# V projection of an encoder layer: eight block products made into seven, with sums of x and w on the other engines

## The reference, cut to what matters

```python
qkv = (x @ w_qkv).reshape(bsz, rows, GRID_W, 3, NA_HEADS, HEAD_DIM)
v = qkv[:, :, :, 2]                       # V of all 16 heads: x (1024 x 1024) times w (1024 x 1024)
...                                       # scores with position bias, softmax over 8 x 16 neighbours
out = pr @ v;  x = layer_norm(ALPHA * x + out @ w_o)     # then gate, embedding, MLP, second norm
```

## Time and profile before

| | us |
|---|---|
| median of 3 runs (1221.72 to 1223.22) | 1222.62 |
| profiled execution, its own time | 1221.3 |
| its span, first to last instruction | 1219.5 |
| V stage, first V matmul to first Q/K matmul | 6.06 to 100.07 |

### The profile page before, as it was taken

One profiled execution on the slowest core, in us unless ns is written; L12 is line 12 of the kernel. 1 busy time (PEld: TensorE's weight loads), 2 busy tenths in 40 slices (PEclk: granted clock), 3 DMA queues, 4 the chain that ended last, 5 costly groups with the idle time before them and its releaser, 6 DMA issues.

```text
span 1219.5 us, 16871 instructions
## 1 busy us (share of the span) xinstructions
PE 1207.0 (99%) x5756; PEld 1012.8 (83%) x5756; DVE 815.8 (67%) x1586; ACT 588.0 (48%) x1139; POOL 211.9 (17%) x264
## 2 busy tenths in 40 slices
PE   9999999999999999999999999999999999999997
PEld 7887888888888888888888888888888888888886
DVE  3311666666667677769677677776764575588786
ACT  3311667677677633244444444444453433333571
POOL 0320555555554433200000000000000000000000
PEclk9999999999999999999999999999999999999999
DMA  8644333433244776683556556465579775778533
GB/s 259 203 127 123 92 94 76 125 111 117 85 121 146 247 221 201 191 312 113 176 211 240 189 208 229 171 239 192 205 250 379 282 271 215 262 242 307 190 104 104
DMA packets 166068, 232.57 MB, mean 191 GB/s; under 512 B 11872, under 2 KB 91872, under 8 KB 164576
## 3 DMA queue, kind: packets, MB, share of 16 engines
q1 hardware_dynamic: 165840, 231.37, 57.4%
q10 hardware_dynamic: 144, 0.13, 0.0%
HBM read 155.83 MB, written 67.29 MB: 183 GB/s over the span
## 4 chain that ended last, share of the span: by engine, by line
PE 96%; DVE 1%; DMA 1%; issue 1%; SPq 0%; ACT 0%; DVEq 0%; ACTq 0%
PE bank L2808 25%; PE bank L2776 25%; PE bank L1263 14%; PE bank L1403 7%; PE bank L1293 7%; PE bank L2732 6%; PE bank L1359 3%; PE bank L1338 3%; PE bank L1324 3%; PE bank L1396 1%; PE bank L1279 1%; PE bank L294 1%; DMA ple_embedding<-embedding_place 0%; DMA k_lo_twice<-k_lo_twice 0%; DMA x_chunk<-in_x 0%
## 5 line engine op out<-in xcount | busy, mean ns | idle before, releaser
L830 POOL TENSOR_TENSOR probabilities<-probabilities,total_reciprocal 128x384 f32<-128x384 f32 (+1 forms) x128 | 99.0, 774 | 153.7 <-DVE total_reciprocal L1148 153.5
L2776 PE MATMUL bank<-x_combination,weight_parts 128*128 128x512 f32 x504 | 118.5, 389 | 0.0
L963 ACT ACTIVATE probabilities<-negated_scores,negated_max 128x384 f32<-128x384 f32 (+1 forms) x128 | 75.5, 590 | 83.0 <-DVE negated_max L1142 82.9
L2776 PEld LDWEIGHTS bank<-x_combination,weight_parts 128*128 128x128 f32 x504 | 94.6, 188 | 19.6
L1263 PE MATMUL bank<-act_T_hi,w_qkv_hi 128*128 128x512 f32 x256 | 102.6, 401 | 0.0
L1263 PE MATMUL bank<-act_T_lo,w_qkv_hi 128*128 128x512 f32 x256 | 100.4, 392 | 0.0
L1263 PE MATMUL bank<-act_T_hi,w_qkv_lo 128*128 128x512 f32 x256 | 100.4, 392 | 0.0
L1142 DVE CUSTOM_DVE_ANT_0 negated_scores<-bank,bias_inner 128x384 f32<-128x384 f32 x96 | 53.2, 554 | 46.5 <-issue 46.0
L2776 PE MATMUL bank<-act_T_hi,weight_parts 128*128 128x512 f32 x240 | 77.3, 389 | 0.0
L2134 ACT ACTIVATE hidden_staging<-hidden_staging 128x512 f32<-128x512 f32 x48 | 30.3, 632 | 94.9 <-DVE hidden_staging L2474 94.9
L2808 PE MATMUL bank<-x_combination,hidden_parts_odd 128*128 128x512 f32 (+1 forms) x324 | 73.1, 381 | 0.0
(11 more groups left out here) (244 smaller groups left out, 2906.8 us busy)
## 6 DMA issues: line engine op xcount, KB each, us to landing
hidden_combinations<-hidden_staging SPq DMA_DIRECT2D x112, 256.0 KB, 2.2
w_ff_in<-in_w_ff SPq DMA_DIRECT2D x27, 1024.0 KB, 7.9
weight_raw<-in_w_ff SPq DMA_DIRECT2D x25, 1024.0 KB, 5.6
weight_raw<-hidden_combinations SPq DMA_DIRECT2D x14, 1024.0 KB, 5.5
hidden_in<-hidden_combinations SPq DMA_DIRECT2D x14, 1024.0 KB, 5.5
v_parts<-v_tile_parts SPq DMA_DIRECT2D x16, 512.0 KB, 3.8
weight_raw<-in_na_w_qkv SPq DMA_DIRECT2D x16, 512.0 KB, 3.8
v_hi_lo<-v_parts SPq DMA_DIRECT2D x8, 1024.0 KB, 5.6
```

The costliest lines, as they stand in the source:

```text
L830: nc.gpsimd.tensor_tensor(prob[:, u % 4, 0:n], prob[:, u % 4, 0:n], recip[:, u % 4:u % 4 + 1].to_broadcast([P, n]), ALU.mult).then_inc(pro ...
L963: nc.scalar.activation(prob[:, u % 4, 0:n], score[:, u % 2, 0:n], ACT.Exp, scale=-1.0, bias=nmax[:, u % 4:u % 4 + 1], accum_out=total[:, u ...
L2776: mm = nc.tensor.matmul(bank, w1_part(wp, u, p)[:, k, :], x_part(ap, p, k), start=(k == 0 and n == 0 and p in (1, 5, 6)), stop=(k == KH4 - ...
```

## The change

x is cut in two by two blocks (inner half by token half), w in two by two (inner half by column half). In place of the eight block products, seven (`V_PRODUCTS`, in the order 1, 2, 5, 6, 7, 3, 4), four of them of sums or differences of blocks. Each product is 4 token tiles (`QUARTER`) by 4 chunks (`KC2`) by 3 passes.

- Product 1 is x's chunks 0 to 3 of the first 512 tokens with `w11`, product 2 chunks 4 to 7 with `w12`; these run as x arrives, chunk by chunk, four tiles instead of six. x is turned one chunk further ahead, into four banks instead of two.
- x operands: ACT also copies the turned chunk raw (`x_raw_copy`); DVE makes `x_sum1` for product 5 and `x_sum3` for product 7; POOL makes those of products 6 and 4, from four chunks each.
- w operands: DVE makes `w21 + w22` for 5 and `w12 - w11'` for 3; POOL makes `w21' = w11 - w21` for 7 and `w11' = w22 - w21'` for 6. `w12` is loaded a second time.
- Every sum is then split: high on ACT, low on DVE, the low parts of x for 7 and 4 on POOL.
- Products 6, 7, 4 share four banks and 5, 3 the other four; DVE adds the banks to the kept product 1 (`v_total`), which gives three quarters of V from SBUF. POOL makes two quarters' low parts.
- SP: no wait on `first_lo` for w's second half; the first pair's Q and K weights come after products 6 and 3; `k_twice(0, 0)` comes before `load_v(0, 0)`.

The core of the diff:

```diff
+V_PRODUCTS = (1, 2, 5, 6, 7, 3, 4)
...
 # POOL
+            for k in range(KC2):
+                pool.wait_ge(x_raw, x_turns(KC2 + k, 1))
+                pool.wait_ge(t1_sum, x_turns(k, 1))
+                pool.wait_ge(x3_sum, k + 1)
+                difference(x_sum_raw[6](k), x_sum_raw[6](k), x_sum_raw[5](k), v_operand_sum)
+                pool.wait_ge(v_operand_sum, 2 * k + 1)
+                difference(x_sum_raw[4](k), x_sum_raw[4](k), x_sum_raw[6](k), v_operand_sum)
+            for k in range(KC2):
+                pool.wait_ge(s1_sum, k + 1)
+                pool.wait_ge(first_lo, w_parts(1, k))
+                difference(w21[0][:, k, :], w11[0][:, k, :], w21[0][:, k, :], v_operand_sum)
+                pool.wait_ge(v_operand_sum, X_SUMS_FIRST + 2 * k + 1)
+                difference(w11[0][:, k, :], w22[0][:, k, :], w21[0][:, k, :], v_operand_sum)
+            for p in (7, 4):
+                for k in range(KC2):
+                    pool.wait_ge(t_hi, x_sum_parts(p, k))
+                    difference(x_part[p](1, k), x_sum_raw[p](k), x_part[p](0, k).bitcast(F32), v_operand_sum)
...
 # DVE
+            for k in range(KC):
+                x_low(k, 0); x_low(k, 1)
+                w_v_low(1 + k // KC2, k % KC2)
+                if k < KC2:
+                    x_sum_first(k, 0); x_sum_first(k, 1)
+                elif k < KC - 1:
+                    x_sum_third(k - KC2)
+            for k in range(KC2):
+                w_sum_first(k)
+                x_sum_low(5, k)
+                w_v_low(5, k)
+                if k == 0:
+                    x_sum_third(KC2 - 1)
+            for n in range(QUARTER):
+                v_low(n)
+            for k in range(KC2):
+                w_sum_fourth(k)
+                w_v_low(6, k)
+                x_sum_low(6, k)
+            for k in range(KC2):
+                w_v_low(7, k)
...
 # PE
+            def v_product(p):
+                for k in range(KC2):
+                    pe.wait_ge(first_lo, w_parts(p, k))
+                    if p in (5, 6):
+                        pe.wait_ge(t_lo, x_sum_parts(p, k))
+                    elif p in (7, 4):
+                        pe.wait_ge(v_operand_sum, X_SUMS_FIRST + x_sum_parts(p, k))
+                    for i in range(QUARTER):
...
+                        v_products(p, i, k)
-            for n in range(FIRST_TILES, V_TILES):
-                v_tile(n)
+            for p in V_PRODUCTS[2:]:
+                v_product(p)
```

More of the change, by code:

```diff
@@ L468, in attention @@
         x_lo = sem("x_lo_done")
+        x3_sum = w4_sum = recip_done
         block = S.block
[L473 to L484, removed]
         def at(name, shape, offset, dt=F32):
             return nc.alloc_sbuf_tensor_at(name, shape, dt, offset=offset)
+        BLOCK = 4 * KC2 * HALF
@@ new lines, in attention @@
+        w_sum1 = raw_and_low("w_v_sum1", [P, KC2, HALF], prob_at)
+        v_first = [at(f"v_product1_{i}", [P, HALF], place)[:, :] for i, place in
+                   enumerate([inner_at + 4 * HALF * i for i in range(QUARTER - 1)] + [score_at])]
+        v_one_five = at("v_products1_5", [P, QUARTER, HALF], prob_at)
+        v_one_six = at("v_products1_6", [P, QUARTER, HALF], prob_at + BLOCK)
+        x_part = {1: lambda part, k: S.act[part][:, k, 0:HALF], 2: lambda part, k: S.act[part][:, KC2 + k, 0:HALF],
+                  3: lambda part, k: S.act[part][:, KC2 + k, HALF:T],
+                  5: lambda part, k: (x_sum_hi[0], x_sum1[1])[part][:, k, :],
+                  6: lambda part, k: x_sum42[1][:, k, HALF:T] if part else x_sum_hi[1][:, k, :],
+                  7: lambda part, k: (x_sum_hi[0], x_sum3[1])[part][:, k, :],
+                  4: lambda part, k: x_sum42[1][:, k, 0:HALF] if part else x_sum_hi[1][:, k, :]}
@@ L652, in _ @@
             sp.sem_inc(out_stored, 16)
[L653 to L656, removed]
+            for m in range(KC):
+                sp.wait_ge(*(chunk_there(m + 4) if m < 4 else second_w_there(m - 4)))
+                load_w_v(m // 2 + KC2 * (m % 2), 1).then_inc(chunk_in[m % 4], 16)
             for c in range(GC):
@@ L845, in copy_bias, with difference, v_low @@
                 nc.gpsimd.tensor_copy(full, src).then_inc(bias_ready, 1)
[L847 to L853, removed]
+            def difference(out, a, b, count):
+                nc.gpsimd.tensor_tensor(out, a, b, ALU.subtract).then_inc(count, 1)
+            def v_low(n):
+                pool.wait_ge(v_hi, n + 1)
+                parts = v_place_of(n)
+                difference(parts[:, :, 1, :], v_source(n), parts[:, :, 0, :].bitcast(F32), v_operand_sum)
+            for k in range(KC2):
[15 more added lines that the diff above has]
+                    difference(x_part[p](1, k), x_sum_raw[p](k), x_part[p](0, k).bitcast(F32), v_operand_sum)
+            for n in range(QUARTER, 2 * QUARTER):
+                v_low(n)
+            for i in range(W_LOWS):
+                split(K_, 0, i)
+            for n in range(2 * QUARTER, 3 * QUARTER):
+                v_low(n)
+            for i in range(W_LOWS):
+                split(Q_, 0, i)
+            pool.wait_ge(v_hi, V_TILES)
+            pool.wait_ge(v_lo, 2 * QUARTER)
             pool.wait_ge(mask_loaded, 16)
@@ new lines, in x_raw_copy, with v_copy @@
+            def x_raw_copy(k, t):
+                act.wait_ge(x_turned, x_turns(k, t))
+                if k == 0 and t:
+                    act.wait_ge(first_step, 2)
+                src = x_chunk_T(k, t)
+                nc.scalar.activation(x_raw_dest(k, t), src if k >= KC2 else src[:, :, QUARTER:GROUPS, :], ACT.Copy)\
+                    .then_inc(x_raw, 1)
+            def v_copy(i):
+                act.wait_ge(v_full, v_done(1, i))
+                nc.scalar.activation(v_first[i], v_first_bank(i), ACT.Copy).then_inc(v_copied, 1)
@@ L1030, in _ @@
                     split(*piece)
-            for i in range(V_PLACES):
+            for i in range(V_COUNTS):
                 act.wait_ge(v_stored[i], V_STORED)
@@ new lines, in w_sum_first, with x_sum_third, w_sum_fourth @@
+            def w_sum_first(k):
+                for half in range(2):
+                    dve.wait_ge(*second_w_there(2 * k + half))
+                nc.vector.tensor_tensor(w_raw[5][:, k, :], w21[0][:, k, :], w22[0][:, k, :], ALU.add).then_inc(s1_sum, 1)
+            def x_sum_third(k):
+                dve.wait_ge(x_raw, x_turns(KC2 + k, 1))
+                nc.vector.tensor_tensor(x_sum_raw[7](k), x_sum_raw[6](k), x_sum_raw[7](k), ALU.subtract).then_inc(x3_sum, 1)
+            def w_sum_fourth(k):
+                dve.wait_ge(w_first_in, 32)
+                dve.wait_ge(v_operand_sum, X_SUMS_FIRST + 2 * (k + 1))
+                nc.vector.tensor_tensor(w12[0][:, k, :], w12[0][:, k, :], w11[0][:, k, :], ALU.subtract).then_inc(w4_sum, 1)
@@ new lines, in v_total @@
+            def v_total(p, i):
+                dve.wait_ge(v_full, v_done(p, i))
+                out, a, bank = {5: (v_one_five[:, i, :], v_first[i], v_second_bank), 6: (v_one_six[:, i, :], v_first[i], v_first_bank),
+                                7: (v_one_five[:, i, :], v_one_five[:, i, :], v_first_bank),
+                                3: (v_one_six[:, i, :], v_one_six[:, i, :], v_second_bank),
+                                4: (v_first[i], v_first[i], v_first_bank)}[p]
+                if p in (5, 6):
+                    dve.wait_ge(v_copied, i + 1)
+                    if p == 6 and i == 0:
+                        dve.wait_ge(v_stored[QUARTER - 1], 16)
+                else:
+                    dve.wait_ge(v_sum, {7: 1, 3: 0, 4: 0}[p] * QUARTER + i + 1)
+                nc.vector.tensor_tensor(out, a, bank(i), ALU.add).then_inc(v_sum, 1)
@@ new lines, in v_products @@
+            def v_products(p, i, k, passes=(0, 1, 2)):
+                bank = v_first_bank(i) if p in (1, 2, 6, 7, 4) else v_second_bank(i)
+                for n in passes:
+                    wp, ap = PASSES[n]
+                    mm = nc.tensor.matmul(bank, x_part[p](ap, k)[:, i * P:(i + 1) * P], (w_high(p), w_low[p])[wp][:, k, :],
+                                          start=(p in (1, 6, 5) and k == 0 and n == 0), stop=(k == KC2 - 1 and n == 2),
+                                          skip_group_check=True)
+                if k == KC2 - 1 and 2 in passes:
@@ new lines, in first_products @@
+                v_products(p, i, k, passes)
+            def v_product(p):
+                for k in range(KC2):
+                    pe.wait_ge(first_lo, w_parts(p, k))
+                    if p in (5, 6):
+                        pe.wait_ge(t_lo, x_sum_parts(p, k))
+                    elif p in (7, 4):
+                        pe.wait_ge(v_operand_sum, X_SUMS_FIRST + x_sum_parts(p, k))
+                    for i in range(QUARTER):
+                        if k == 0:
+                            if p == 5:
+                                pe.wait_ge(x_lo, x_turns(KC - 1, 1))
+                            elif p == 6:
```

(4 more changed lines are left out.)

409 lines of the change are left out of this document (268 added, 141 removed).

## The result

The changed kernel takes 1225.26 us, median of 20 runs (1223.56 to 1226.40), against 1222.65 (1220.77 to 1224.59) before: ratio 1.0021, 95% interval 1.0015 to 1.0028. The forecast was 1225.7 and slower. The profiled execution took 1225.05, its span is 1223.3; before they were 1221.3 and 1219.5.

The account below looks back on a forecast made before the run. PE was taken to bound the kernel (96% of the last chain). Stage end 30.55 + 33.95 + 5.44 + 32.65 + 0.6 = 103.2, +3.1; 1221.3 + 3.1 = 1224.4, median 1.3 above: 1225.7 us, range 1212.5 to 1234.

Parts of the forecast that it names:

- Matmuls and tail: V stage and behind it: 336 V matmuls, 48 fewer, worth -10.9 us; moved loads behind the stage cost 0.
- Start: While x arrives: chunk 2's turn released at 11.50, then 3.61 a chunk, chunk 7's turn over at 30.55.
- The price of a POOL pass: Operand sums in the V stage: each POOL subtraction costs a DVE pass with two SBUF inputs 1.11 us.
- price by full blocking: Same sums by the skill's rule: a POOL subtraction would cost 1.26 and the sum 1.8 more.
- How many: DVE's chain to product 6's third chunk: 12 POOL passes stand between DVE passes; that chunk starts at T + 33.95.
- T: The moment chunk 7's turn on PE is over, forecast at 30.55.
- The end: End of the V stage: forecast at 103.2 against 100.07, +3.1 us.
- A: Rival, V stage: DVE and POOL do not hold each other, PE bound by its own work; -9.7, 1212.9; chance 0.14.
- B: Rival, product 7's four POOL low parts wait until product 6's sums are made: chain 4.4 shorter, -1.3, 1221.3; chance 0.20.
- C: Rival, while x arrives: four chunks with POOL working (4 to 7) each 0.7 late; 1228.5; chance 0.07.
- D: Rival, PE's pauses lower its granted clock: three chunks take twice their 2.72, +8.2, 1233.9; chance 0.07.

Follow-up runs that it names:

- e2: Changed kernel with all twenty-four POOL subtractions for V's operands made by DVE; 1220.10 us, ratio 0.9969 to the kernel before.
- e1: Changed kernel with POOL's sixteen sums on 8 columns, not 512, and its four low parts for product 7 put last; 1212.65 us, ratio 0.9910 to the kernel before.
- e3: Changed kernel with one wait more, putting POOL's four low parts for product 7 behind DVE's; 1223.57 us, ratio 1.0001 to the kernel before.
- e6: As e1, but with POOL's sixteen sums on 256 columns in place of 8; 1217.73 us, ratio 0.9957 to the kernel before.
- e4: Changed kernel with POOL's passes shared out by what they read, POOL keeping fourteen and DVE making ten; 1217.75 us, ratio 0.9951 to the kernel before.

## Why the prediction was right, step by step

**Matmuls and tail.** Right: 336 V matmuls, and behind the stage 1119.5 against 1119.4, though the transfers moved as the prediction said. The DMA issues of SP, and PE's first product with V:

```profile
116.99 0.52 SPq L713 DMA_DIRECT2D k_hi_twice<-k_hi_twice  x1
...
120.21 1.01 SPq L738 DMA_DIRECT2D v_hi_lo<-v_parts  x1
```
```profile
L1631 PE MATMUL bank<-prob_T_hi,v_hi_lo x10: 224/366/422, 134.3 to 148.9; 128*128 128x256 f32 x4, 128*128 128x384 f32 x4, 128*128 128x128 f32 x2
```

V's load moved from 4.4 to 16.4 us behind the stage's end, and PE came to V 30.5 behind it, as before.

**Start.** Nearly right, 0.8 too early: PE's first turn for chunk 2 was released by the DMA at 12.07, not 11.50, and chunk 7's turn was over at 31.37, not 30.55. Of this 0.57 is the landing, which differs by more than that between the profiles (11.53 in e2); from the end of chunk 2's turn to that of chunk 7's it took 18.45 where 18.20 was forecast.

```profile
12.07 1.09 PE L1537 MATMUL bank<-identity,x_chunk 128*128 128x128 f32 x8 [0.70 <-DMA w_v<-in_na_w_qkv]
```

**The price of a POOL pass.** 1.11 forecast from one pair of rows of another kind and size; 1.09 measured. That it came so near from a copy of half the pitch is partly luck. This is the term that decides the sign: at nothing, the forecast gave 1212.9 and e1 measured 1212.65. The Trainium skill ("SBUF — State Buffer", section "Who interferes with whom") says that a DVE instruction with two inputs in SBUF contends with a GpSimd instruction that reads SBUF and one with at most one such input, outside its 2-port modes, does not; the trace agrees on both, 1.75 against 0.69 and four bank passes in 2.47 to 2.48 beside POOL. The price by full blocking that the prediction quotes, 1.26, is more than the 1.09 measured.

**How many.** Twelve POOL passes on the chain were forecast; the timeline has twelve DVE passes of 1.60 to 1.79 between 39.40 and 64.9, eight in product 5 and four in product 6. Product 6's third chunk starts 34.27 behind the turn of chunk 7 (65.64 - 31.37), where 33.95 was forecast. One term's words don't give its number: three pitches and a POOL pass behind T + 2.4 make T + 5.3, and only two pitches and a pass make the T + 4.75 that the sum uses. The trace bears out the number: the first sum of w starts at 35.11 and is held, 1.78, so the next pass starts at 36.81, as behind an unheld one at T + 4.84.

**The end.** 103.84 against 103.2: 0.8 from the start, 0.3 from the chain, and 0.5 the other way in the last 168 matmuls, which have no restarts. In the profiled executions the change cost 3.75 against a forecast of 3.1; in the medians 2.6, because the kernel before had been profiled in a run 1.35 below its median and the changed one only 0.2 below. So it is in part luck that the median came within 0.5 us of the forecast: the stage cost 0.65 more than forecast, and the changed kernel's profiled run lay 1.1 nearer its median than was assumed.

**Rivals.** A (no hold) was wrong, but its time, 1212.9, is near the 1212.65 of e1, where the hold is gone. B's 4.4 was mis-sized: moving those passes gives 2.4, since PE's own pace then sets product 6 (e3). C hardly came: of its 2.8 there are 0.25 from chunk 2's turn to chunk 7's. D was half right: the clock did fall, but in this kernel it cost nothing (below). PE's pauses were put at 12 us and are 8.9; 1.8 of the difference is the slow chunk (4.59 in place of 2.75), which filled part of one, and the rest is about what the restarts cost beside the idle time that is shown (seven of 0.26, the estimate of e6).

## What to carry to other kernels

Before handing elementwise work to POOL to relieve DVE, look at what DVE reads at that moment: beside DVE passes with two SBUF inputs a POOL subtraction of 128x512 cost DVE 1.09, more than the 0.60 that DVE would have needed to do it itself, while beside DVE passes that read a bank it was free. So hand POOL the passes that fall beside bank reads or idle time, and give the rest back. And price a move on the chain that ends last, with the next bound beside it: four passes off DVE's chain were worth 4.4 there and 2.4 to the kernel.

## What the runs showed that was not expected

The granted clock fell for one short stretch in three of the seven new kernels, and only one of them lost time by it. In the changed kernel the pauses begin at 37.70; PE is busy 3.12 of 5.30 and 2.98 of 5.00, and then the mean granted clock from 48 to 53 is 0.66 (the stretches above): most matmuls of that chunk are 0.43 apart in place of 0.23, near the lower level of 1.2 GHz. PE ended that chunk and still waited 0.48 for DVE:

```profile
53.07 0.50 PE L1551 MATMUL bank<-w_v_hi,x_sum_hi 128*128 128x512 f32 x1 [0.48 <-DVE w_v_sum_lo L1282]
```

In e3 the same happened one chunk later: 3.06, 3.04 and 3.05 of 5.00 busy, then

```profile
53.00:58.00 5.00, 4.67 (x13) 3.22 (x14) 4.90 (x9) 3.85 (x9) 2.70 (x2) 0.66 0.67 231
```

with 12 matmuls in 4.50; its next operands came at 57.7, when PE was just through. In both the next stretch is at 1.00 again. In e2 it fell behind a single pause of 2.72, with PE busy throughout from 44 to 49.9, and there no operand was late behind it, so it cost 1.4 us. In e4 a pause of 2.54 left it at 1.00, and in e6, busy 4.56, 4.20 and 3.62 of 5.00, it stayed at 1.00 throughout. The Trainium skill ("TensorE: Matmul & The Clock Gate", section "A second HAM failure mode: psum-queue depth-cycling") tells of frequent small pauses between groups of matmuls that make the clock swing; here the pauses were 1.3 to 2.0 us in the changed kernel and in e3, and one of 2.72 in e2. What exactly tips it, these runs do not separate.
